# Streaming a value table two tiles to a transfer, with two neighbouring rows on each partition

## The reference, cut to what matters

```python
expert = (e1 * PEER_NKEYS + e2).reshape(T, n_sel)      # PEER_NKEYS = 128
...
act = jax.nn.gelu(jnp.einsum('td,tkd->tk', xb, u_tab[eb]))
return jnp.einsum('tk,tkd->td', gb * act, v_tab[eb])
...
x = x + g2 * peer(hn2, ...)
return rmsnorm(x, final_norm_w), ...
```

## Time and profile before

| | |
|---|---|
| three runs | 3525.66, 3522.31, 3512.60 us |
| median | 3522.31 us |
| span of the profiled execution | 3512.3 us |
| the profiled execution's own time | not listed apart; the fastest run is 3512.60 us |
| PE, DVE, ACT, POOL busy | 91%, 78%, 40%, 55% of the span |
| mean granted TensorE clock | 0.976 |
| DMA, mean over the span | 321 GB/s, 1127.33 MB |

### The profile page before, as it was taken

The page is one execution under the profiler, slowest core; times in us unless marked ns, Lnnn a source line. Parts: engine busy times, 40 slices in busy tenths (PEclk is TensorE's granted clock), DMA queues, the critical chain, the costliest instruction groups (busy, mean ns, idle before and its releaser), DMA issues.

```text
span 3512.3 us, 57824 instructions
## 1 busy us (share of the span) xinstructions
PE 3196.7 (91%) x18338; PEld 2567.2 (73%) x18338; DVE 2751.0 (78%) x5867; ACT 1387.6 (40%) x3099; POOL 1947.2 (55%) x1504
## 2 busy tenths in 40 slices
PE   7999999999999989988999999999989999998655
PEld 4777766666666668767878888888877888877554
DVE  3333357998988887889899999999999887666776
ACT  4444311333332221587555555555555565000110
POOL 0000013565577763345776776767767775676776
PEclk9999999999999999999999999999999999999899
DMA  8444455788899998778999999999999999999998
GB/s 268 150 149 150 139 165 165 254 264 285 260 323 328 322 340 306 248 252 304 396 390 396 392 387 397 371 365 396 387 346 392 375 409 404 386 410 408 407 408 345
DMA packets 429325, 1127.33 MB, mean 321 GB/s; under 512 B 41968, under 2 KB 166256, under 8 KB 429168
## 3 DMA queue, kind: packets, MB, share of 16 engines
q0 software_dynamic: 204800, 745.10, 56.7%
q1 hardware_dynamic: 219600, 370.51, 29.6%
q10 hardware_dynamic: 4768, 9.96, 0.8%
HBM read 1098.82 MB, written 26.62 MB: 320 GB/s over the span
## 4 chain that ended last, share of the span: by engine, by line
DVE 18%; issue 15%; DMA 14%; PE 12%; POOL 5%; ACT 1%; POOLq 0%; DVEq 0%; ACTq 0%; SPq 0%
DMA rows<-in_peer_u,eidx 10%; DVE rows L1773 7%; PE vacc L2377 6%; POOL rows L1571 3%; DMA W<-in_peer_v,eidx 2%; DVE oh1w L1854 2%; PE vacc L2291 2%; DMA rows<-in_peer_v,eidx 2%; PE scat L2311 2%; POOL W L1571 1%; DVE oh L1849 1%; DVE eidx L1667 1%; DVE htok L1783 1%; PE scat L2364 1%; DVE ti L1718 1%
## 5 line engine op out<-in xcount | busy, mean ns | idle before, releaser
L1571 POOL DMA_INDIRECT rows<-in_peer_u,eidx x1072 | 1416.5, 1321 | 846.7 <-DVE dots L1773 501.1
L2377 PE MATMUL vacc<-W,vbuf 128*128 (+1 forms) x6144 | 1425.6, 387 | 32.6 <-DMA vbuf<-in_peer_v 23.6
L1773 DVE CUSTOM_DVE_ANT_0 rows<-rows,htok 128x1024 f32<-128x1024 f32 x1072 | 1326.4, 1264 | 157.7 <-DMA rows<-in_peer_u,eidx 149.1
L2377 PEld LDWEIGHTS vacc<-W,vbuf 128*128 128x128 f32 x6144 | 1156.8, 192 | 183.2 <-issue 34.0
L2111 ACT ACTIVATE oh<-iota,e2s 128x128 bf16<-128x128 f32 x1536 | 486.5, 391 | 17.3 <-DVE wpart L1825 10.0
L928 PE MATMUL vacc<-W 128*128 128x384 f32 x1280 | 430.8, 493 | 1.2 <-ACTq L805 1.2
L1550 POOL TENSOR_TENSOR hot<-hot,ccid 128x864 f32<-128x864 bf16 x68 | 130.7, 1927 | 530.1 <-DVE hot L1758 528.8
L928 PEld LDWEIGHTS vacc<-W 128*128 128x128 f32 x1280 | 241.8, 192 | 168.7 <-issue 6.8
L2118 ACT ACTIVATE W<-scat 128x256 f32 (+1 forms) x320 | 122.9, 384 | 563.5 <-PE scat L2364 560.3
L2114 ACT ACTIVATE oh<-oh,ones 128x512 bf16<-128x512 bf16 x384 | 277.2, 722 | 12.5
L1854 DVE TENSOR_TENSOR oh1w<-oh,wpart 128x768 bf16<-128x768 bf16 x384 | 241.8, 630 | 44.3 <-PE scat L2364 24.4
(11 more groups left out here) (346 smaller groups left out, 3281.0 us busy)
## 6 DMA issues: line engine op xcount, KB each, us to landing
vbuf<-in_peer_v SPq DMA_DIRECT2D x384, 512.0 KB, 6.7
W<-in_w_in SPq DMA_DIRECT2D x80, 512.0 KB, 6.6
W<-in_wq SPq DMA_DIRECT2D x64, 512.0 KB, 4.3
vbuf<-in_w_ada SPq DMA_DIRECT2D x9, 2048.0 KB, 8.0
rows<-in_peer_u,eidx POOLq DMA_INDIRECT x1072, 7.3
W<-in_w_in SPq DMA_DIRECT2D x16, 1024.0 KB, 6.3
W<-in_w_ada SPq DMA_DIRECT2D x3, 2048.0 KB, 15.9
W<-in_w_out SPq DMA_DIRECT2D x12, 512.0 KB, 6.6
```

The lines of the kernel that those rows point to most:

```text
L1571: g.indirect_dma_start(row_of[s], None, table[:, :], bass.IndirectOffsetOnAxis(ap=picked, axis=0)).then_inc(landed[s], 16)
L1773: v.tensor_tensor_reduce(row_of[s], row_of[s], htok[:, home, :], 1.0, 0.0, ALU.mult, ALU.add, dots_of(t)[:, c:c + 1]).then_inc(used, 1)
L2377: mm = pe.matmul(vacc[:, k, :], vbuf[:, s, k * P:(k + 1) * P], W[:, e1, :].rearrange("p o t -> p (o t)"), start=(clear and s == 0 and k % ...
```

## The change

V's stream takes two tiles at once: one transfer of 1 MB takes the rows 256j to 256j + 255 of V, with the rows 256j + 2p and 256j + 2p + 1, 8 KB that lie together, on partition p, into two neighbouring buffers. It waits until both buffers have been used, and counts on one semaphore for two buffers. PE waits for it before the first tile of a pair only. Expert e now lies on partition (e >> 1) & 127 of tile ((e >> 8) << 1) | (e & 1), and picks_low makes these two numbers with four operations where there were two. The gathered rows are not touched.

```diff
-        h_in, v_in = [sem("h_in0"), sem("h_in1")], [sem(f"v_in{i}") for i in range(VB)]
+        h_in, v_in = [sem("h_in0"), sem("h_in1")], [sem(f"v_in{i}") for i in range(VB // 2)]
...
                     with sp.Fori(lo, hi) as i:
-                        for s in range(VB):
-                            sp.wait_ge(v_used, g * NKEY + i * VB + (s + 1))
-                            sp.dma_start(vbuf[:, s, :], I["peer_v"][bass.ds((i * VB + s) * P, P), :]).then_inc(v_in[s], 16)
+                        for s in range(0, VB, 2):
+                            sp.wait_ge(v_used, g * NKEY + i * VB + (s + 2))
+                            src = I["peer_v"][bass.ds((i * VB + s) * P, 2 * P), :].rearrange("(p r) d -> p (r d)", r=2)
+                            sp.dma_start(vbuf[:, s:s + 2, :].rearrange("p r d -> p (r d)"), src).then_inc(v_in[s // 2], 16)
...
-                    v.tensor_scalar(n[0], e, 7, None, ALU.logical_shift_right)
-                    dl_(v.tensor_scalar(n[1], e, NKEY - 1, None, ALU.bitwise_and))
+                    v.tensor_scalar(n[1], e, 8, 1, ALU.logical_shift_right, ALU.logical_shift_left)
+                    dl_(v.tensor_scalar(n[0], e, 1, None, ALU.bitwise_and))
+                    dl_(v.tensor_tensor(n[0], n[0], n[1], ALU.bitwise_or))
+                    dl_(v.tensor_scalar(n[1], e, 1, NKEY - 1, ALU.logical_shift_right, ALU.bitwise_and))
...
                         for s in range(VB):
-                            pe.wait_ge(v_in[s], g * (16 * NKEY // VB) + i * 16 + (q4 * (16 * QB // VB) + 16))
+                            if s % 2 == 0:
+                                pe.wait_ge(v_in[s // 2], g * (16 * NKEY // VB) + i * 16 + (q4 * (16 * QB // VB) + 16))
```

## The result

The changed kernel takes 3589.1 us (median of 4 runs, 3577.5 to 3595.3), the kernel before beside it 3524.0 (3512.6 to 3526.2): a ratio of 1.0188, 95% interval 1.0169 to 1.0207. It is slower, as forecast, but by 65 us and not by 30: 3552 was predicted, and 3589 lies inside the range of 3508 to 3625, at more than twice the forecast step.

The account below looks back on a forecast made before the run. The prediction took PE at its own pace as the bound, with DVE and DMA nearly full too. Its terms, 12 + 9 + 5 + 3 + 5 - 4 = +30 us on a median of 3522.3, gave 3552 us, range 3508 to 3625.

Parts of the forecast that it names:

- The landing: V load on SP's queue: 1 MB lands 7.85 us after issue, bounds 7.0 to 9.3, against 7.8 us of cover.
- R1: Rival: each 8 KB row of V travels as two packets, landing 9.3 us, about 3670 us; chance 0.10.
- Term 1: V stream beside the scatter, up to 2985 us: late pair loads cost PE 80 x 0.15 = +12 us (0 to 120).
- term 3: V loads behind four 1 MB transfers in SP's queue: each 1.2 us later, +5 us (0 to 11).
- Term 2: V stream after the scatter, 2985 to 3240 us: PE loses 23 us, 14 covered, +9 us (0 to 23, or 46).
- the 14 us of cover: End of V stream: 11 gathers under way in POOL's slots hold 14 us of DMA work, deducted from PE's 23 us.
- Term 4: picks_low on DVE, two to four operations: 0.6 us a call, 6 calls, +3 us (2 to 5).
- Term 5: POOL's row gathers beside larger V bursts: delay spreads more and DVE waits for rows, +5 us (below 0 to 46).
- R4: Rival: the V burst starves DVE of gathered rows, some 3590 us; chance 0.10.
- Term 6: DMA engines, fewer packets: 18 us saved per engine, counting only after 2985 us, -4 us (0 to -18).
- R3: Rival: DMA is the real bound and the saved 18 us come out in full, 3504 us; chance 0.10.
- R2: Rival: the V load stays hidden, landing in 7.7 us or less, about 3530 us, no change; chance 0.22.

Follow-up runs that it names:

- late_singles: The changed kernel, but the last 64 tiles of V loaded one by one, with PE waiting for each: 3552.0 us, ratio 1.0105 to the kernel before.
- longer_picks: The kernel before with picks_low in four operations that give the old numbers, reads and waits unchanged: ratio 0.9995.
- two_halves: The kernel before with both 512 KB loads of a pair issued together once the second buffer is free: 3559.4 us against 3518.8, ratio 1.0125.
- one_later: The kernel before with single 512 KB loads of V, each issued one tile later: ratio 1.0082.

## Why the prediction was off, step by step

**The landing (7.85 us): nearly right.** 8.0 to 8.3, worked out from packet times that the trace of before shows. The packet stays whole (R1 is out), and its 0.32 us stands (0.326 measured).

**Term 1, A: +12; A is +30.8.** The mechanism is right, the size is not. PE's waits for V grew by 24.5 us. 5.9 of them belong to term 3 (the two large transfers in A), and 18.6 to this term: 33 waits of 0.56 us at the mean, where I had 80 of 0.15. The landing was 0.2 to 0.5 us over the cover of 7.8 and not 0.05. Fewer than half of the 80 chances were late at all. That PE's other pauses lengthen the cover fits this, but was not tested. Where a landing and its cover are equal, a few tenths of a microsecond are the whole term. The 6.3 us of A that are left are no waits for V; where they come from is open, and A's own spread is as large.

**Term 2, B: +9. This is the step that failed.** The stall of 23 us for PE was fair: the ordinary waits of 17.8 us, with what the tiles behind them lose, cost 21.4 us, in single waits of 1.2 to 1.8 us for the most part. But the 14 us of cover taken off it don't exist. I read the earlier trace rows as DVE waiting for PE, with the ring of gather slots as the slack behind it, and counted 11 gathers under way as 14 us of DMA work done ahead. The trace has DVE busy up to the gate and there 0.7 us after PE, so the slack was 0.7 us and not 14. The ring gave next to none: when the stream ended, the changed kernel's POOL had issued 3 gathers more than before and then stood with full slots, and the stretch behind is 275.1 us, where it was 272.8. late_singles shows it in one number: 28.6 us less in B, none of it back in C.

**Term 3, SP's large transfers: +5; about +17.** In B they cost 11.5 us more, in A PE's waits behind them grew by 5.9. I counted four of 1 MB and overlooked the sample tokens' x (L1519 before, 256 KB in packets of 256 B, behind 512 KB of sums), as it was hidden before: 4.0 us of delay there became 12.8. The other two places in B grew by 2.7 us together, near the 1.2 each; the two in A grew by 5.9 and not by 2.4. I also had three of PE's five waits before at the transfers of 1 MB; it is four, and the fifth is the sample tokens'. With this, B is 21.4 + 8.8 + 2.7 = 32.9 of 32.7.

**Term 4, picks_low: +3.** A call grew by 0.6 us, as forecast, though in other parts: the two added operations take 0.29 and 0.23 us and start 0.04 us after the one before them; no run shows the 0.08 us a wait. longer_picks: nothing to be seen of it in the time (A 1336.0 in both).

**Term 5, the burst: +5.** In the changed kernel DVE's waits for rows did not grow in the stage (111.7 us against 115.1). That PE's waits slow DVE's work first fits, but is not shown by itself. two_halves shows the size that stands behind: about 8 us of its 16 in A. The terms don't add; the larger hides the other. R4 as a mechanism exists, and did not decide.

**Term 6, the DMA time saved: -4.** The packets did get 2.4% cheaper per KB. As PE and not the DMA sets the pace, nothing of it comes out: R3 is out, as the DMA share fell instead (0.99 for 1.01 in 1750 to 2000, 0.97 for 0.99 in 2000 to 2250).

**The rivals.** The time is the one that R4 gave (3590), and that is chance: it came by the forecast's own mechanism, the waits of PE for V in A and B alike, and DVE's waits for rows did not grow. R2's own terms (4 + 5 + 3 + 5 - 4) add up to 3535 us and not to 3530; nothing hangs on it.

The Trainium skill ("DMA: Bandwidth & Descriptors", section "Anatomy of one DMA") gives its formula as a fit for transfers issued from GpSimd, and these are SP's. It would have had 4.4 us for 1 MB; measured are 8.0 to 8.3 beside the gathers. Its section "SWDGE vs HWDGE vs iDMA" prefers packets up to 4096 B. Half the packets for the same bytes shows rows of 8 KB travelling whole here.

## What to carry to other kernels

Joining two transfers halves the number of waits and takes away a buffer's worth of lead; compare the landing of the joined one, from packet times and the turns of the other queue, with the time from its issue to its need, and treat anything closer than its spread as late. A delay of one engine before a gate is only covered as far as another engine comes to the gate later still (here DVE, 0.7 us later); what is under way in the queues is no cover. Look whether the waiting engine is idle or busy just before the gate. List every transfer in the queue of the moved one, the well hidden ones too: they are hidden by the lead that goes, and in one_later 16 of the 20 us by which PE's waits for V grew in B were there.

## What the runs showed of the hardware

- Reading every second row of 4 KB of V instead of a run of rows cost 41.5 to 41.6 ns per KB of SP's packets instead of 40.8, and 14 us of the kernel, through DVE's waits for its own gathers.
- The same 1 MB beside the gathers: with rows of 8 KB the kernel is 39 us quicker than with rows of 4 KB, though a packet saves only 8 ns of 334.
- In the changed kernel PE's waits of 9.48 and 8.45 us were followed by a stretch at a granted clock of 0.50 (1.2 GHz; 3094.5 to 3100 and 3214.6 to 3217), and the four tiles behind them took 3.1 and 2.6 us longer than behind a wait of 1.59 us, where the clock stayed at 1.00.
- On one chip it took 294 to 302 us from the gate to the end, and on the others 270 to 276. In C, longer_picks had a DMA rate of 340 GB/s and a granted clock of 0.82 there, the kernel before 387 and 0.93 elsewhere; A was 1336.0 us in both. Why is open.
